# Half of a Strassen-Winograd feed-forward's weight sums moved from GpSimd to accumulating DMAs, half to VectorE

## Chip, core and metric

One core of one Trainium2 chip runs the whole program. The metric is the device time of one execution in microseconds (us), the median of three. TensorE is called PE below, VectorE DVE, ScalarE ACT, GpSimd POOL, and SyncE, which only issues transfers, SP.

## What is computed

The reference is two transformer blocks over x of 512 positions by 1024 features in fp32, with causal recurrences and several kinds of attention. The change touches the feed-forward of the first block, which stands in it twice:

```
def _swiglu(h, w_gate, w_up, w_down):
    g = h @ w_gate
    u = h @ w_up
    return (silu(g) * u) @ w_down        # 1024 -> 2816 -> 1024
x = x + mix                               # recurrent mixer (layer 0), stick-breaking attention (layer 1)
x = x + _swiglu(rmsnorm(x) , ...)
```

## The kernel before

**Layout.** Everything is transposed: features on the 128 partitions, the 512 positions along the free axis. X holds the 1024 features as 8 chunks. A full-precision product is three PE passes over fp32r operands: each operand is split in a high part (ACT copies it to fp32r: Wh, Hh, Fh, Yh) and a low part (DVE subtracts: Wl, Hl, Fl, Yl), and PE adds high by low, low by high and high by high.

**Two output units at a time.** An output unit is 128 features of the gate or of the up projection. A pair h is one gate unit and the up unit of the same features. Instead of 2 by 2 by 2 block products, a pair is computed with seven (Strassen-Winograd): the weights are cut in A11, A12 (gate, two halves of the 1024 inputs) and A21, A22 (up), the activations in B11, B12, B21, B22 (inputs by halves of the positions). Weight operands of the seven products are A11, A12, A22 and four sums: S1 = A21 + A22, S2 = S1 - A11, S3 = A11 - A21, S4 = A12 - S2. T1 to T4 are the matching sums of activations, made once for each norm. One block product is 4 steps of 3 matmuls with 256 columns, so a pair has 84 matmuls. The 44 pairs come in four parts: gu0a (12 pairs), gu0b (10), gu1a (12), gu1b (10). Each is followed by its down projection, down0a and so on. The a parts begin while the output projection of the mixer (rg_out, sb_out) runs out, with the norm; the b parts begin behind a down projection.

**Who does what for pair g+1 while PE multiplies pair g.** SP's `load_pairs` (L393 to L413) loads the gate and the up row, 512 KB each, in raw_w (parity 1 in Wr, parity 0 in scr). POOL's `weight_sums` (L527 to L553) makes S3, S1, S2, S4 in this order, one tensor_tensor of 128x512 each; the first two read both rows, and each waits until its target is free, which DVE's low splits tell it. `sum_hi` (ACT, L1378 to L1386) makes the high part of A (A11 and A12 in one, 128x1024), A22, S1 to S4, and `sum_lo` (DVE, L1997 to L2002) the low part. `split_at` gives the count of splits at which each block is ready. DVE also evacuates the products: four reads of 128x256 (`read` L2086, `rows_right` L2096), a scaling (`rows_left` L2091), act by up (L2102) and the low part of the result (L2106).

**Order on DVE in `iteration(g)`** (L2112 to L2160), which is written out by hand: rows_right(g-2), S4(g-1) low, act_by_up(g-2), S3(g+1) low, Y low (g-2), first read of g, A(g+1) low, third_read(g-1), S1(g) low, rows_left(g-1), A22(g+1) low, second read of g, S2(g+1) low. On PE (`pair`) the order is S3, A12, A11, S1 of the pair before, A22, S2, S4 of the pair before; S2 waits for the first read, S4 for third_read.

**Norm.** In the eight steps m of the mixer's output projection (`out_proj`, ACT L1388, DVE L2037) DVE adds unit m to X, ACT and DVE make the quarters T1 to T4 of chunk m in fp32 and split them (`even_quarters`, `odd_quarters`, `even_lo`, `odd_lo`), ACT squares the chunk, and POOL's `add_square` (L518 to L525) adds the squares up. The inputs' halves are taken as even and odd chunks, so each half is complete only at the end.

Of the kernel before, what the change touches and what calls it, by code (L numbers as in the profile page):

```python
# [16 lines left out]
ACT = mybir.ActivationFunctionType  # L17
ALU = mybir.AluOpType
# [115 lines left out]
OUT_KC = {"rg_out": KD, "sb_out": KD, "even_out": MIXC, "odd_out": MIXC}  # L134
PAIR_OUT = {"gu0a": "rg_out", "gu0b": "down0a", "gu1a": "sb_out", "gu1b": "down1a"}
# [35 lines left out]
def program(nc, a):  # L171
    with ExitStack() as ctx:
# [47 lines left out]
        def part(off, n, w):  # L220
# [38 lines left out]
        raw_w = [(part(7168, KD, P), part(8192, KD, P)),  # L259
                 tuple(Wr[:, q, 0:KD * P].rearrange("p (k c) -> p k c", k=KD) for q in range(2))]  # L260
        raw_rows = raw_w
        raw_w = [[r.rearrange("p (j e) c -> p e j c", e=2) for r in two] for two in raw_w]
        sum3, sum2 = scr[:, 9216:9728], scr[:, 9728:10240]
# [17 lines left out]


# [64 lines left out]
        sum_ok, p2_ok, dc_ok, e_ok = sem("sum_ok"), sem("p2_ok"), sem("dc_ok"), sem("e_ok")  # L347
        dh_ok, rt1_ok = sem("dh_ok"), sem("rt1_ok")
# [6 lines left out]

        def block4(t):
            return t.rearrange("p (j c) -> p j c", j=4)
# [9 lines left out]
        def weight_source(tag, par):  # L367

            if tag == "A":
                return raw_w[par][0]  # L370
            if tag == "A22":
                return raw_w[par][1][:, 1]
            return block4({"S1": sum1[par], "S2": sum2, "S3": sum3, "S4": sum4[par]}[tag])

        def weight_view(w, tag):

            return weights(w, tag).rearrange("p (e j c) -> p e j c", e=2, j=4) if tag == "A" else block4(weights(w, tag))
# [3 lines left out]
        def _(sp):  # L381
# [11 lines left out]
            def load_pairs(name, b, row, pairs):  # L393

                p0, landed = PAIR0[name], 8 * b - SKIP[name]
                rows = a[f"w{KD}"].rearrange("u p (k c) -> u p k c", c=P)

                def load_pair(h, par):
                    for q in range(2):
                        sp.wait_ge(w_in[q], 16 * h + landed)  # L400
                        if h == 0:
                            if name.endswith("a"):
                                sp.wait_ge(x_ok, X0[PAIR_OUT[name]] + 1)
                            else:
                                sp.wait_ge(w_lo, b - 7)
                        elif h == 1:
                            sp.wait_ge(w_lo, b - 1 + q)
                        else:
                            sp.wait_ge(w_lo, b + 2 + q if h == 2 else 6 * h + (b - 12 + 2 * q))
                            sp.wait_ge(sum_ok, 4 * h + (4 * p0 - 4))  # L410
                        sp.dma_start(raw_rows[par][q], rows[2 * h + (row + q)]).then_inc(w_in[q], 16)
                for h in range(pairs):
                    load_pair(h, h % 2)  # L413
# [23 lines left out]
            for name, kc, n in STREAM:  # L437
# [12 lines left out]
                if name in DOWNS:  # L450
                    gu = name.replace("down", "gu")
                    p0, b, pairs = PAIR0[gu], UNIT0[gu], kc
                    sp.wait_ge(w_lo, b + 6 * pairs - 5)
                    sp.wait_ge(sum_ok, 4 * (p0 + pairs))
                    sp.dma_start(Wr[:, 0, 0:kc * P], w[row]).then_inc(w_in[0], 16)
                    sp.wait_ge(w_lo, b + 6 * pairs)
                    sp.dma_start(Wr[:, 1, 0:kc * P], w[row + 1]).then_inc(w_in[1], 16)
                    it0 = 1
                if name in ("rg_out", "sb_out"):
                    load(u0, 0, w[row])  # L460
                    load(u0 + 1, 1, w[row + 1])
                    sp.wait_ge(w_hi, u0 + 1)
                    sp.dma_start(place(Wr, CORNER, KD), w[row + 2].rearrange("p (s c) -> p s c", s=2)).then_inc(w_in[0], 16)
                    load(u0 + 3, 1, w[row + 3])
                    it0 = 2
# [12 lines left out]
        def _(pool):  # L478
# [39 lines left out]
            def add_square(norm, m):  # L518

                pool.wait_ge(sq_ok, SQUARES[norm] + m + 1)  # L520
                if m == 0:
                    pool.tensor_copy(acc[:, :], sq[:, 0, :]).then_inc(acc_ok, 1)
                else:
                    pool.wait_ge(acc_ok, SQUARES[norm] + m)
                    pool.tensor_tensor(acc[:, :], acc[:, :], sq[:, m % 2, :], ALU.add).then_inc(acc_ok, 1)  # L525

            def weight_sums(name, h, par, steps=(0, 1, 2, 3)):  # L527

                b, p0 = UNIT0[name], PAIR0[name]
                gate, up = raw_w[par]  # L530
                lo_at = {"S3": 6 * h + (b - 7), "S1": 6 * h + (b - 5), "S2": 6 * h + (b - 3), "S4": 6 * h + (b - 2)}
                if isinstance(h, int) and h < 2:
                    corner = b - 5 if name.endswith("a") else b - 1 + h
                    lo_at = {"S3": b + 1 if h else b - 7, "S1": corner, "S2": b + 4 if h else b - 7, "S4": b - 7}
                done = 4 * h + 4 * p0
                for step in steps:
                    if step == 0:
                        landed = 16 * h + (8 * b - SKIP[name] + 16)
                        pool.wait_ge(w_in[0], landed)
                        pool.wait_ge(w_in[1], landed)  # L540
                        pool.wait_ge(w_lo, lo_at["S3"])
                        pool.tensor_tensor(block4(sum3), gate[:, 0], up[:, 0], ALU.subtract).then_inc(sum_ok, 1)
                    if step == 1:
                        pool.wait_ge(w_lo, lo_at["S1"])
                        pool.tensor_tensor(block4(sum1[par]), up[:, 0], up[:, 1], ALU.add).then_inc(sum_ok, 1)
                    if step == 2:
                        pool.wait_ge(w_lo, lo_at["S2"])
                        pool.wait_ge(sum_ok, done + 2)
                        pool.tensor_tensor(block4(sum2), block4(sum1[par]), gate[:, 0], ALU.subtract).then_inc(sum_ok, 1)
                    if step == 3:  # L550
                        pool.wait_ge(w_lo, lo_at["S4"])
                        pool.wait_ge(sum_ok, done + 3)
                        pool.tensor_tensor(block4(sum4[par]), gate[:, 1], block4(sum2), ALU.subtract).then_inc(sum_ok, 1)  # L553

            def ffn(layer, norm):
                for part_, chunks in (("a", FFA), ("b", FFB)):
                    name = f"gu{layer}{part_}"
                    if part_ == "a":
                        for m in range(6):
                            add_square(norm, m)  # L560
                        weight_sums(name, 0, 0, (0, 1))
                        add_square(norm, 6)
                        weight_sums(name, 0, 0, (2, 3))
                        add_square(norm, 7)
                    else:
                        weight_sums(name, 0, 0)
                    weight_sums(name, 1, 1)
                    with pool.Fori(1, chunks // 2) as it:
                        for par in range(2):
                            weight_sums(name, 2 * it + par, par)  # L570

            ffn(0, "ffn0")
            ffn(1, "ffn1")

# [767 lines left out]
        def _(act):  # L1342
# [35 lines left out]
            def sum_hi(name, h, tag, par, used):  # L1378

                p0 = PAIR0[name]  # L1380
                if tag in ("A", "A22"):
                    act.wait_ge(w_in[tag == "A22"], 16 * h + (8 * UNIT0[name] - SKIP[name] + 16))
                else:
                    act.wait_ge(sum_ok, 4 * h + (4 * p0 + {"S3": 1, "S1": 2, "S2": 3, "S4": 4}[tag]))
                act.wait_ge(w_used, used)
                act.activation(weight_view(Wh, tag), weight_source(tag, par), ACT.Copy).then_inc(w_hi, 1)  # L1386

            def out_proj(name, norm, pairs_in=None):  # L1388
# [6 lines left out]
                for m in range(KD - 2 if norm == "final2" else KD):  # L1395
# [14 lines left out]
                    if pairs_in:  # L1410
                        j, e = m // 2, m // 2 % 2
                        act.wait_ge(x_ok, x0 + m + 1)
                        if m % 2 == 0:
                            both = tE[e].rearrange("p (a b) -> p a b", b=256)[:, 0:3:2, :]
                            act.activation(both, X[:, m, :].rearrange("p (a b) -> p a b", b=256), ACT.Copy,
                                           scale=v_col(norm, m)).then_inc(xe2_ok, 1)
                            if m == 6:
                                sum_hi(pairs_in, 0, "A", 0, u0 + 7)
                            square(norm, m, X[:, m, :])
# [4 lines left out]
                        else:  # L1424
                            chunk_hi(Hh[:, m, :], X[:, m, :], v_col(norm, m))
                            square(norm, m, X[:, m, :])
# [482 lines left out]
        def _(dve):  # L1909
# [87 lines left out]
            def sum_lo(name, h, tag, par):  # L1997
# [3 lines left out]
                dve.tensor_tensor(weight_view(Wl, tag), weight_source(tag, par), weight_view(Wh, tag).bitcast(F32), ALU.subtract)\  # L2001
                    .then_inc(w_lo, 1)  # L2002

# [853 lines left out]
```

## Time and profile before

| | us |
|---|---|
| median of 3 runs (lowest, highest) | 1937.99 (1937.77, 1940.19) |
| the profiled execution | 1939.89 |
| its span, first to last instruction | 1938.2 |
| PE, DVE, ACT, POOL busy in it | 1877.3, 1377.6, 944.6, 452.3 |
| transfers | 174.02 MB, mean 90 GB/s |

The profiled execution took 1.7 us more than its span and 1.9 more than the median. Durations on DVE overlap a little in the trace: the next instruction's row starts some 0.07 before the end of the one before, so what an instruction costs its engine is read as the distance of two starts.

### The profile page before, as it was taken

What the parts mean: (1) busy time and instruction counts of PE and PEld (TensorE: products, weight loads), DVE (VectorE), ACT (ScalarE), POOL (GpSimd) and SP (SyncE); (2) the same over time, 40 slices, a digit from 0 to 9 for tenths busy, and PEclk for the clock granted to TensorE, in tenths of its full rate; (3) what the DMA queues carried; (4) which work ended last, traced back from release to release, by engine and by line L of the source; (5) the groups of instructions that cost most, each with busy time, mean ns of one, the idle gap of its engine ahead of it and who ended that gap; (6) DMA issues with size and microseconds to landing.
All of it is one profiled execution on the core that took longest, in us unless ns stands there. A gap on an engine that the chain in (4) does not pass through costs nothing.

```text
span 1938.2 us, 30375 instructions
## 1 busy us (share of the span) xinstructions
PE 1877.3 (97%) x10662; PEld 1563.2 (81%) x10662; DVE 1377.6 (71%) x2106; ACT 944.6 (49%) x1573; POOL 452.3 (23%) x426
## 2 busy tenths in 40 slices
PE   9999799999999999979999999999999999999998
PEld 7787689989988777769988998876777887777777
DVE  7687899739965677689964996666667565656553
ACT  6476466415543444546632555345655344444442
POOL 3011555126400000056502530000002045341000
PEclk9999899999999999989999999999999999999999
DMA  7334233233222222223223313211123233232322
GB/s 255 101 96 127 86 98 97 82 114 89 78 96 79 74 61 62 63 87 98 87 98 98 108 57 119 77 55 60 52 86 95 87 89 85 76 87 80 93 82 76
DMA packets 53874, 174.02 MB, mean 90 GB/s; under 512 B 7392, under 2 KB 15712, under 8 KB 53776
## 3 DMA queue, kind: packets, MB, share of 16 engines
q1 hardware_dynamic: 47408, 162.62, 26.8%
q0 software_dynamic: 6368, 10.13, 2.3%
q8 instruction: 57, 0.93, 0.2%
q14 instruction: 41, 0.34, 0.1%
HBM read 168.51 MB, written 4.21 MB: 89 GB/s over the span
## 4 chain that ended last, share of the span: by engine, by line
PE 73%; DVE 11%; issue 4%; ACT 1%; DVEq 0%; ACTq 0%
PE ps L656 15%; PE ps L658 15%; PE ps L657 15%; DVE Wl L2001 4%; PE ps L944 3%; PE tr L910 3%; PE ps L742 3%; PE ps L744 3%; PE ps L743 3%; PE sc L742 2%; PE sc L744 2%; PE sc L743 2%; PE sc L867 2%; DVE Fl L2001 1%; DVE gs L2086 1%
## 5 line engine op out<-in xcount | busy, mean ns | idle before, releaser
L656 PE MATMUL ps<-Hl,Wh 128*128 128x512 f32 x784 | 329.1, 420 | 0.0
L1354 ACT ACTIVATE Wh<-Wr 128x1024 fp32r<-128x1024 f32 (+2 forms) x172 | 195.6, 1139 | 258.7 <-PE ps L658 226.9
L658 PE MATMUL ps<-Hh,Wh 128*128 128x512 f32 x784 | 307.7, 392 | 0.0
L657 PE MATMUL ps<-Hh,Wl 128*128 128x512 f32 x784 | 307.1, 392 | 0.0
L1915 DVE TENSOR_TENSOR Wl<-Wr,Wh 128x1024 fp32r<-128x1024 f32 (+2 forms) x172 | 231.3, 1345 | 102.3 <-ACT Wh L1354 100.8
L656 PE MATMUL ps<-Yl,Wh 128*128 128x512 f32 (+1 forms) x648 | 254.1, 392 | 11.1 <-DVE Wl L1915 7.7
L657 PE MATMUL ps<-Yh,Wl 128*128 128x512 f32 (+1 forms) x648 | 250.8, 387 | 0.0
L658 PE MATMUL ps<-Yh,Wh 128*128 128x512 f32 (+1 forms) x648 | 250.4, 386 | 0.0
L656 PEld LDWEIGHTS ps<-Hl,Wh 128*128 128x128 f32 x784 | 147.8, 188 | 40.3 <-issue 11.1
L742 PE MATMUL ps<-Hl,Wh 128*128 128x256 f32 x528 | 153.8, 291 | 24.9 <-DVE gs L2086 18.8
L2001 DVE TENSOR_TENSOR Wl<-scr,Wh 128x512 fp32r<-128x512 f32 (+1 forms) x132 | 174.5, 1326 | 1.0 <-ACT Wh L1386 1.0
L658 PEld LDWEIGHTS ps<-Hh,Wh 128*128 128x128 f32 x784 | 147.5, 188 | 33.2
L657 PEld LDWEIGHTS ps<-Hh,Wl 128*128 128x128 f32 x784 | 148.1, 189 | 25.8 <-issue 0.5
L656 PEld LDWEIGHTS ps<-Yl,Wh 128*128 128x128 f32 x648 | 122.8, 189 | 38.9 <-issue 9.7
L744 PE MATMUL ps<-Hh,Wh 128*128 128x256 f32 x528 | 150.1, 284 | 0.0
L743 PE MATMUL ps<-Hh,Wl 128*128 128x256 f32 x528 | 150.1, 284 | 0.0
L658 PEld LDWEIGHTS ps<-Yh,Wh 128*128 128x128 f32 x648 | 122.9, 190 | 24.7
L657 PEld LDWEIGHTS ps<-Yh,Wl 128*128 128x128 f32 x648 | 123.0, 190 | 24.0 <-issue 0.7
L1386 ACT ACTIVATE Wh<-scr 128x512 fp32r<-128x512 f32 (+1 forms) x132 | 91.6, 699 | 99.4 <-PE ps L744 72.7
L742 PEld LDWEIGHTS ps<-Hl,Wh 128*128 128x128 f32 x528 | 101.6, 192 | 33.0 <-DVE gs L2086 20.7
L1565 ACT ACTIVATE scr<-tr 128x768 f32<-128x768 f32 (+1 forms) x96 | 72.4, 754 | 74.9 <-PE tr L910 74.2
L2001 DVE TENSOR_TENSOR Wl<-Wr,Wh 128x1024 fp32r<-128x1024 f32 (+1 forms) x88 | 104.6, 1193 | 4.7 <-ACT Wh L1386 4.5
(405 smaller groups left out, 4326.1 us busy)
## 6 DMA issues: line engine op xcount, KB each, us to landing
Wr<-in_w SPq DMA_DIRECT2D x184, 512.0 KB, 3.6
Wr<-in_w SPq DMA_DIRECT2D x32, 768.0 KB, 4.1
scr<-in_w SPq DMA_DIRECT2D x44, 512.0 KB, 3.6
Wr<-in_w SPq DMA_DIRECT2D x16, 640.0 KB, 3.8
scr<-in_rpb POOLq DMA_DIRECT2D x128, 24.0 KB, 2.1
X<-in_x SPq DMA_DIRECT2D x8, 256.0 KB, 4.2
Wr<-in_wri SPq DMA_DIRECT2D x4, 512.0 KB, 3.5
out_t<-X SPq DMA_DIRECT2D x8, 256.0 KB, 2.5
```

The lines of the kernel that those rows point to most:

```text
L656: pe.matmul(bank[:, 0:n], hi, rl[:, k, :], start=(k == 0), stop=False)
L657: pe.matmul(bank[:, 0:n], lo, rh[:, k, :], start=False, stop=False)
L658: return pe.matmul(bank[:, 0:n], hi, rh[:, k, :], start=False, stop=(k == kc - 1))
L742: pe.matmul(out, hi[:, cs], tl, start=(begins and j == 0), stop=False, skip_group_check=True)
L743: pe.matmul(out, lo[:, cs], th, start=False, stop=False, skip_group_check=True)
L744: mm = pe.matmul(out, hi[:, cs], th, start=False, stop=(j == 3), skip_group_check=True)
L910: mm = pe.transpose(tr[:, h, n * P:(n + 1) * P], Pb[:, 2 * (t % 2) + h, n * P:(n + 1) * P], ident[:, :])
L1354: act.activation(place(Wh, slot, kc), place(Wr, slot, kc), ACT.Copy).then_inc(w_hi, 1)
L1386: act.activation(weight_view(Wh, tag), weight_source(tag, par), ACT.Copy).then_inc(w_hi, 1)
L1565: act.activation(PT.rearrange("p h (c q) -> p h c q", c=4)[:, :, cs[0]:cs[0] + n, b * P:(b + 1) * P], tr[:, :, 0:n * P].rearrange("p h (c ...
L1915: dve.tensor_tensor(place(Wl, slot, kc), place(Wr, slot, kc), place(Wh, slot, kc).bitcast(F32), ALU.subtract)\
L2001: dve.tensor_tensor(weight_view(Wl, tag), weight_source(tag, par), weight_view(Wh, tag).bitcast(F32), ALU.subtract)\
```

## The change

S1 and S3 are no longer computed by an engine. SP loads one operand into the place of the sum (sum1 with A21, sum3 with A11), and POOL issues a DMA with `accum_op=ALU.add` that reads the other operand from HBM again and adds it to what lies in SBUF (A22 to sum1, A21 to sum3). [...] S2 and S4 are made by DVE, in `second_sum` and `fourth_sum`. `add_square` of the two feed-forward norms moves from POOL to DVE. The halves of the inputs are now chunks 0 to 3 and 4 to 7, so that a sum is one contiguous half row; the mixer's output units are taken in the order CHUNK so that the pairs of halves still come side by side. sum3 has two buffers instead of one. Of the up row only the right half is loaded plainly. DVE gets two small tensor_scalar instructions for negated gains.

```
+CHUNK = [0, 4, 1, 5, 2, 6, 3, 7]
-        sum3, sum2 = scr[:, 9216:9728], scr[:, 9728:10240]
+        raw_a = [scr[:, 7168:8192], Wr[:, 0, 0:2 * S]]
+        raw_22 = [scr[:, 8192:8704], Wr[:, 1, 0:S]]
+        sum3, sum2 = [scr[:, 8704:9216], scr[:, 9216:9728]], scr[:, 9728:10240]
+        def summed(p0, h, par):
+            return 8 * (h - par) + (8 * p0 + 16)
# SP, load_pairs: for each pair
+                def blocks(h, par):
+                    gate, up = rows[2 * h + row], rows[2 * h + (row + 1)]
...
+                        sp.wait_ge(w_lo, b + lo_at["S3"])          # of pair h - 2
+                    sp.dma_start(sum3[par], gate[:, 0:S]).then_inc(s3_in[par], 16)
...
+                        sp.wait_ge(w_lo, b + lo_at["A"])
+                        sp.wait_ge(sum_ok, 2 * (p0 + h - 1))
+                    sp.wait_ge(w_in[0], 16 * h + landed)
+                    sp.dma_start(raw_a[par], gate).then_inc(w_in[0], 16)
...
+                        sp.wait_ge(w_lo, b + lo_at["A22"])
+                    sp.wait_ge(w_in[1], 16 * h + landed)
+                    sp.dma_start(raw_22[par], up[:, S:2 * S]).then_inc(w_in[1], 16)
+                blocks(0, 0)
                 for h in range(pairs):
...
+                        sp.wait_ge(w_lo, b + split_at(h - 2, pairs)["S1"])
+                    sp.dma_start(sum1[par], rows[2 * h + (row + 1)][:, 0:S]).then_inc(s1_in[par], 16)
+                    if h + 1 < pairs:
+                        blocks(h + 1, 1 - par)
# POOL: the four tensor_tensor of weight_sums go, and
+                def third(h, par):
+                    pool.wait_ge(s3_in[par], summed(p0, h, par))
+                    pool.dma_start(sum3[par], a[f"w{KD}"][2 * h + (row + 1)][:, 0:S], accum_op=ALU.add).then_inc(s3_ok[par], 16)
+                third(0, 0)
+                for h in range(pairs):
+                    par = h % 2
+                    pool.wait_ge(s1_in[par], summed(p0, h, par))
+                    pool.dma_start(sum1[par], a[f"w{KD}"][2 * h + (row + 1)][:, S:2 * S], accum_op=ALU.add).then_inc(s1_ok[par], 16)
+                    if h + 1 < pairs:
+                        third(h + 1, 1 - par)
# DVE
+            def second_sum(name, h, par):
...
+                dve.wait_ge(s1_ok[par], summed(p0, h, par))
...
+                dve.tensor_tensor(sum2, sum1[par], raw_a[par][:, 0:S], ALU.add).then_inc(sum_ok, 1)
+            def fourth_sum(name, h, par):
+                dve.wait_ge(sum_ok, 2 * h + (2 * PAIR0[name] + 1))
+                dve.tensor_tensor(sum4[par], sum2, raw_a[par][:, S:2 * S], ALU.add).then_inc(sum_ok, 1)
@@ iteration
                     if more:
+                        second_sum(name, g + 1, 1 - par)
                         sum_lo(name, g + 1, "A", 1 - par)
...
                     if more:
+                        fourth_sum(name, g + 1, 1 - par)
                         sum_lo(name, g + 1, "S2", 1 - par)
@@ odd_quarters: one scalar_tensor_tensor of 512 columns becomes two of 256
@@ out_proj
+                    if pairs_in and nrm:
+                        add_square(nrm, m)
```

## Rows read from the trace of the kernel before

**Rows 1.** The page, its head and busy times.

```profile
span 1938.2 us, 30375 instructions
PE 1877.3 (97%) x10662; PEld 1563.2 (81%) x10662; DVE 1377.6 (71%) x2106; ACT 944.6 (49%) x1573; POOL 452.3 (23%) x426
```

**Rows 2.** Busy time by window: begin, length, engines, granted PEclk, DMA share, GB/s.

```profile
222.00:260.00 38.00, 29.95 (x202) 27.85 (x201) 32.36 (x35) 19.89 (x32) 24.76 (x16) 0.91 0.27 83
...
236.00:353.00 117.00, 109.34 (x855) 105.28 (x856) 114.56 (x136) 70.92 (x112) 63.93 (x42) 0.99 0.27 81
```

**Rows 3.** Timeline of PE's weight loads, one pair: start, us, what, [idle before].

```profile
330.42 0.19 PEld L743 LDWEIGHTS ps<-Eh,Wl 128*128 128x128 f32 x1
330.54 0.19 PEld L744 LDWEIGHTS ps<-Eh,Wh 128*128 128x128 f32 x1
...
331.46 0.19 PEld L742 LDWEIGHTS ps<-Hl,Wh 128*128 128x128 f32 x1 [0.74 <-DVE gs L2086]
...
342.52 0.19 PEld L742 LDWEIGHTS ps<-Hl,Wh 128*128 128x128 f32 x1 [0.73 <-DVE gs L2086]
```

**Rows 4.** Timeline of DVE in the same pair, and after POOL's last sum.

```profile
326.47 1.78 DVE L2001 TENSOR_TENSOR Fl<-scr,Fh 128x512 fp32r<-128x512 f32 x1
...
329.11 1.97 DVE L2001 TENSOR_TENSOR Wl<-Wr,Wh 128x1024 fp32r<-128x1024 f32 x1
...
331.34 0.67 DVE L2001 TENSOR_TENSOR Wl<-Wr,Wh 128x512 fp32r<-128x512 f32 x1
...
332.27 1.78 DVE L2001 TENSOR_TENSOR Wl<-Wr,Wh 128x512 fp32r<-128x512 f32 x1
...
350.29 0.68 DVE L2106 TENSOR_TENSOR Yl<-ht,Yh 128x512 fp32r<-128x512 f32 x1
350.89 0.41 DVE L2086 TENSOR_TENSOR sq<-ps,rstd 128x256 f32<-128x256 f32 x1
351.23 1.21 DVE L2001 TENSOR_TENSOR Wl<-Wr,Wh 128x1024 fp32r<-128x1024 f32 x1
352.36 0.41 DVE L2086 TENSOR_TENSOR gs<-ps,acc 128x256 f32<-128x256 f32 x1
```

**Rows 5.** Timeline of POOL, one sum of the same pair.

```profile
332.09 1.41 POOL L545 TENSOR_TENSOR Wr<-scr 128x512 f32<-128x512 f32 x1 [2.09 <-DVE Wl L2001]
```

**Rows 6.** Timeline of PE's weight loads at the start of gu0a.

```profile
226.65 0.28 PEld L742 LDWEIGHTS ps<-Hl,Wh 128*128 128x128 f32 x1 [3.43 <-issue]
...
234.12 0.19 PEld L742 LDWEIGHTS sc<-El,Fh 128*128 128x128 f32 x1 [1.53 <-DVE El L2035]
...
241.54 0.19 PEld L742 LDWEIGHTS sc<-El,Fh 128*128 128x128 f32 x1 [1.03 <-DVE Fl L2001]
...
247.95 0.19 PEld L742 LDWEIGHTS ps<-Hl,Wh 128*128 128x128 f32 x1 [1.58 <-DVE Wl L2001]
```

**Rows 7.** DMA issues: queue, count, KB each, median us from issue to landing.

```profile
scr<-in_w SPq DMA_DIRECT2D x44, 512.0 KB, 3.6
...
out_t<-X SPq DMA_DIRECT2D x8, 256.0 KB, 2.5
scr<-d_rel POOLq DMA_DIRECT2D x8, 192.0 KB, 3.6
...
scr<-d_memk POOLq DMA_DIRECT2D x2, 512.0 KB, 5.2
...
scr<-in_rope POOLq DMA_DIRECT2D x1, 512.0 KB, 4.3
```

**Rows 8.** Timelines of POOL and DVE in the neighbourhood attention's first bias loads.

```profile
1489.88 8.42 POOL L611 DMA_DIRECT2D scr<-in_rpb  x16 [81.37 <-PE sc L915]
```

**Rows 9.** Timeline of DVE in the same stretch.

```profile
1492.64 0.68 DVE L2291 TENSOR_TENSOR Yl<-acc,Yh 128x512 fp32r<-128x512 f32 x1
...
1494.35 1.76 DVE L1915 TENSOR_TENSOR Wl<-Wr,Wh 128x1536 fp32r<-128x1536 f32 x1 [1.02 <-ACT Wh L1354]
```

**Rows 10.** Timeline of SP's queue in the pair of rows 3.

```profile
331.14 3.30 SPq L411 DMA_DIRECT2D Wr<-in_w  x2
```

More of the change, by code:

```diff
@@ L280, in program @@
         ps += [ctx.enter_context(nc.psum_tensor(f"ps{i}", [P, S], F32)) for i in range(6, 8)]
+        first_row, _rows = {}, {}
+        for _name, _k, _n in STREAM:
+            first_row[_name] = _rows.get(_k, 0)
+            _rows[_k] = first_row[_name] + _n
         def place(w, slot, kc):
@@ L367, in weight_source @@
         def weight_source(tag, par):
[L369 to L377, printed above, removed]
+            return {"A": raw_a[par], "A22": raw_22[par], "S1": sum1[par], "S2": sum2, "S3": sum3[par], "S4": sum4[par]}[tag]
+        def summed(p0, h, par):
+            return 8 * (h - par) + (8 * p0 + 16)
         @block.sync
@@ L393, in load_pairs @@
             def load_pairs(name, b, row, pairs):
[L395 to L411, printed above, removed]
@@ L460, in _ @@
                     load(u0, 0, w[row])
-                    load(u0 + 1, 1, w[row + 1])
+                    load(u0 + 1, 1, w[row + CHUNK[1]])
                     sp.wait_ge(w_hi, u0 + 1)
-                    sp.dma_start(place(Wr, CORNER, KD), w[row + 2].rearrange("p (s c) -> p s c", s=2)).then_inc(w_in[0], 16)
-                    load(u0 + 3, 1, w[row + 3])
-                    it0 = 2
+                    sp.dma_start(place(Wr, CORNER, KD), w[row + CHUNK[2]].rearrange("p (s c) -> p s c", s=2)).then_inc(w_in[0], 16)
+                    for m in range(3, KD):
+                        load(u0 + m, m % 2, w[row + CHUNK[m]])
+                    continue
                 with sp.Fori(it0, n // 2) as it:
@@ L516, in _ @@
             store_mem_v(1)
[L518 to L570, printed above, removed]
@@ L572, in _, with weight_sums @@
-            ffn(0, "ffn0")
-            ffn(1, "ffn1")
+            def weight_sums(name):
+                p0, row, pairs = PAIR0[name], first_row[name], FFA if name.endswith("a") else FFB
+                def third(h, par):
[3 more added lines that the diff above has]
+                for h in range(pairs):
+                    par = h % 2
+                    pool.wait_ge(s1_in[par], summed(p0, h, par))
+                    pool.dma_start(sum1[par], a[f"w{KD}"][2 * h + (row + 1)][:, S:2 * S], accum_op=ALU.add).then_inc(s1_ok[par], 16)
+                    if h + 1 < pairs:
+                        third(h + 1, 1 - par)
@@ L575, in _ @@
+            for name in ("gu0a", "gu0b", "gu1a", "gu1b"):
+                weight_sums(name)
             pool.wait_ge(w_used, UNIT0["down1b"])
@@ L2000, in sum_lo @@
                 dve.wait_ge(w_hi, b + split_at(h, pairs)[tag])
-                dve.tensor_tensor(weight_view(Wl, tag), weight_source(tag, par), weight_view(Wh, tag).bitcast(F32), ALU.subtract)\
+                dve.tensor_tensor(weights(Wl, tag), weight_source(tag, par), weights(Wh, tag).bitcast(F32), ALU.subtract)\
                     .then_inc(w_lo, 1)
+            def second_sum(name, h, par):
+                p0 = PAIR0[name]
+                if not (isinstance(h, int) and h == 0):
+                    prior = h - 1 if not isinstance(h, int) or h > 1 else 0
+                    dve.wait_ge(w_lo, UNIT0[name] + split_at(prior, 99)["S2"])
+                    dve.wait_ge(sum_ok, 2 * h + 2 * p0)
+                dve.wait_ge(s1_ok[par], summed(p0, h, par))
+                dve.wait_ge(w_in[0], 16 * h + (8 * UNIT0[name] - SKIP[name] + 16))
+                dve.tensor_tensor(sum2, sum1[par], raw_a[par][:, 0:S], ALU.add).then_inc(sum_ok, 1)
+            def fourth_sum(name, h, par):
+                dve.wait_ge(sum_ok, 2 * h + (2 * PAIR0[name] + 1))
+                dve.tensor_tensor(sum4[par], sum2, raw_a[par][:, S:2 * S], ALU.add).then_inc(sum_ok, 1)
             def even_quarters(nrm, m):
@@ L2055, in out_proj @@
                         bank = m if name in ("rg_out", "sb_out") and m < 4 else b0 + m % 2
-                        dve.tensor_tensor(X[:, m, :], X[:, m, :], ps[bank][:, :], ALU.add).then_inc(x_ok, 1)
+                        c = CHUNK[m] if name in ("rg_out", "sb_out") else m
+                        dve.tensor_tensor(X[:, c, :], X[:, c, :], ps[bank][:, :], ALU.add).then_inc(x_ok, 1)
                     if name in ("rg_out", "sb_out") and m == 0:
@@ L2063, in out_proj @@
                     if pairs_in and m == 6:
+                        second_sum(pairs_in, 0, 0)
                         if not nrm:
@@ L2460, in _ @@
             rg_lo(RB - 1)
+            for norm, home in MINUS.items():
+                dve.tensor_scalar(vec[:, VEC[home]:VEC[home] + KD], vec[:, VEC[norm]:VEC[norm] + KD], -1.0, None, ALU.mult)\
+                    .then_inc(neg_ok, 1)
             out_proj("rg_out", "ffn0", "gu0a")
```

70 lines of the change are left out of this document (46 added, 24 removed).

## The prediction

> **What bounds the kernel now.** The page comes first: PE is busy for 97% of the span, so little is to be had from anything else [rows 1]. But the change touches one stage only, so I read that stage by windows: over the pairs of gu0a DVE is busy for 114.56 of 117 us, PE for 109.34, POOL for 63.93 [rows 2]. There DVE, not PE, is full. The timeline of PE's weight loads says what that costs. Loads follow each other every 0.12 us (330.42 to 330.54), so the 84 matmuls of a pair need 10.08; yet the same product begins at 331.46 and at 342.52, 11.06 apart [rows 3]. The missing 0.98 is PE waiting for a read by DVE before S4 (0.92 between two loads), and a shorter wait before S2. I count 28 of the 44 pairs with this wait: 8 in each a part, 6 in each b part.
>
> Why is DVE full? Its timeline shows a low split of 128x512 at 0.67 (S1, 331.34) and the next, same shape, at 1.78 (A22, 332.27) [rows 4]. In between POOL's sum begins at 332.09 [rows 5]. Each of POOL's four sums in a pair holds one DVE instruction up. Behind POOL's last sum the same list runs free, and distances of starts there give net prices [rows 4]: 0.60 for 512 columns (350.29 to 350.89), 0.34 for 256 (to 351.23), 1.13 for 1024 (to 352.36). A pair has seven, five and one of these: 7 x 0.60 + 5 x 0.34 + 1.13 = 7.03. The other 4.03 of 11.06 are POOL's.
>
> **The change, part by part.**
>
> *POOL's sums go, two come to DVE.* 7.03 + 2 x 0.60 = 8.23 us of DVE in a pair, under PE's 10.08. I laid DVE's list against PE's: the first read can be done 2.3 us before S2 needs it, third_read, now with second_sum and A low ahead of it, 1.6 before S4. So both waits go: 28 x 0.98 = **-27**.
>
> *The fronts of gu0a and gu1a.* PE waits 3.43 for the first half of the inputs, 1.53 for the second, 1.03 for S3 of pair 1 and 1.58 for the second read [rows 6]. All stand behind DVE work that POOL holds up, about 1.1 each time; I replay the list with free prices and the new instructions. X's chunk 6 is then added 2.5 us sooner and the first wait goes; of the 1.53 some 0.7 go, the third goes, of the fourth 1.4; and 2.1 of small waits in the next two pairs: 3.4 + 0.7 + 1.1 + 1.4 + 2.1 = 8.7, twice: **-18**. The granted clock is 0.91 over 222 to 260 [rows 2], with two stretches of half speed that begin behind these waits; without them some 3 come back: **-3**. Last pairs of the parts and starts of the b parts have waits for DVE of 0.3 to 0.6: **-2**.
>
> *add_square on DVE.* 16 at 0.60, in steps where POOL's adds cost DVE 1.1 each: nothing net, inside the -18. If that cover is gone they cost up to 10.
>
> *Signs, CHUNK, contiguous halves, the split scalar_tensor_tensor (+0.1 x 8), two negations:* same operations on other addresses; nothing, covered by DVE's slack of 1.9 in a pair, at most 2 without it.
>
> *SP and POOL queues.* SP issues five loads in a pair for two, at about 0.33 each; its queue starts 0.06 behind its release (A low ends 331.08, SP 331.14 [rows 4, 10]) and otherwise idles. Transfers grow from 1.0 to 1.75 MB in a pair; the DMA share of 0.27 [rows 2] becomes about 0.5. Issuing from POOL does not hold DVE: beside POOL's issues from 1489.88 to 1498.30 [rows 8] a 512 instruction takes 0.68 and a 1536 one 1.76 [rows 9].
>
> *The new chain.* This is the uncertain term. sum1 of pair g+2 may be loaded only when S1 low of g is done; the load lands, POOL issues the accumulating DMA, it lands, second_sum, A low and third_read of the next iteration follow, then S1 low of g+1, which releases the next load. So the chain has one period to run in:
> c = L1 + L2 + hand-offs 0.3 + DVE 2.8 (0.66 + 1.13 + 0.34 + 0.68).
> L1, a load of 256 KB by SP: 2.5 (a store of that size) to 3.6 (512 KB) [rows 7]; I take 2.7, near the row of its size, plus a little for sum3's load right behind. L2, 256 KB through POOL with an addition, is in no row. From below: 192 KB plain takes 3.6 with others ahead, and a first one some 0.4 less, so 3.2. From above: 512 KB plain in company, 5.2 [rows 7], and a row that nothing excludes could be longer, 6. I take 4.3, the 512 KB plain row, as the addition moves two operands. That gives c = 10.1. The gate and up loads for the pair after, 768 KB, are issued about 2.3 after sum1's and run against the accumulation: +0.2. **c = 10.3**, against 10.08. 36 pairs follow the chain: 36 x 0.22 = **+8**. At each part's start it begins late: by the replay of gu0b's start S1 low of pair 0 ends 5.5 before the moment at which second_sum of pair 2 would have to begin for PE's S4 not to wait, so S4 waits L1 + L2 + 0.3 - 5.5 = 1.8, four times: **+7**.
>
> On that price the Trainium skill speaks against the change: "Collectives: The Full Stack" (The bandwidth ceiling: the fold count and why AG ≠ RS ≠ AR) has an adding DMA read two sources through one ring, so that it moves at half the rate of a copy. No row here shows an addition; by that rule L2 is that of a 512 KB copy, the 4.3 taken above.
>
> **Sum.** -27 - 18 - 3 - 2 + 8 + 7 = -35 on the profiled execution's 1939.9: 1905. The median of the runs lies 1.9 lower, so **1903**. The formula for other prices: -50 + 4 (L1 + L2 - 5.2) + 36 max(0, c - 10.08). It is back at zero at c of 11.15, L1 + L2 of 8.0.
>
> **Rivals.**
> *A, slower: the sum1 chain becomes the bound.* Place: second_sum waits for s1_ok, and everything behind it on DVE, third_read above all, for which PE waits. Price: 40 us for each us of c. It decides from c = 11.15 up. With L1 = 3.6 and L2 = 5.2, both rows, c = 11.9 and -50 + 14 + 65 = +29: 1967. With 3.0 and 5.5 c is 11.6: +18, 1956. For it: every row of L2 is a guess by size, three DMAs compete. Against: between the bursts the engines stand idle. Chance 0.22.
> *B, the chain has room.* L2 = 3.2 to 3.6: c = 9.2 to 9.6, no stall in the loop, starts cost 2 to 4: -47, 1891. For it: the row of 192 KB. Chance 0.25. The skill's "DMA: Bandwidth & Descriptors" (Anatomy of one DMA — SWDGE (gpsimd) path) would put this DMA at 2.0 + bytes/436e3, an estimate of 2.6, and so speaks for B; the rows for 192 KB are a us longer, so it gets no more.
> *C, POOL's hold on DVE stays in another form* (descriptor writing, DMA writes into buffers being read), or add_square and the new order undo the fronts: about what it was, 1930 to 1942. Against: rows 8 and 9. Chance 0.06.
> *The forecast,* c within about 0.6 above PE's 10.08: 1893 to 1923. Chance 0.47.
>
> **Numbers.** Faster by over 0.2% (about 4 us, what a measurement of this kernel can tell): forecast, B and half of C, less a margin: 0.74. Slower by over 0.2%: A, 0.22. Within: 0.04. The range takes in B's 1890, the forecast, and of A all but its end: 1887 to 1960.
>
> **What would show it.** Right: no POOL tensor_tensor between 190 and 1165; all 512-column low splits at 0.67 to 0.69; DVE busy about 8.2 in a pair; pairs 10.1 to 10.4 apart; the load that waited 3.43 waits under 1. The accumulating DMA lands 4.3 behind its issue. If c is over: DVE idles ahead of second_sum, released by a DMA, and PE's S4 waits for third_read as before, with a period equal to c. I am wrong if pairs stand over 11 apart, if low splits still take 1.78, or if the accumulating DMA lands after more than 5.3.

## The result, and the profile after

The kernel after the change takes 1965.58 us in the median of four runs (1964.4 to 1969.48), the kernel before beside it 1937.88 (1937.24 to 1940.19). The ratio is 1.0144, 95% interval 1.0127 to 1.0162: slower by 27.7 us, where I had forecast 35 us faster. It is rival A that came true, with its place and almost its price. The profiled execution is the one of 1964.4 us, with a span of 1962.7, 24.5 more than the span before.

The page after, its head, busy times and the rows of the DMA issues (count, KB each, median us to landing), to be held against [rows 1, 7]:

```profile
span 1962.7 us, 30196 instructions
PE 1875.2 (96%) x10662; PEld 1567.3 (80%) x10662; DVE 1279.7 (65%) x2220; ACT 951.7 (48%) x1573; POOL 233.6 (12%) x322
...
Wr<-in_w SPq DMA_DIRECT2D x66, 256.0 KB, 3.0
...
scr<-in_w POOLq DMA_DIRECT2D x44, 256.0 KB, 6.5
Wr<-in_w POOLq DMA_DIRECT2D x44, 256.0 KB, 5.7
```

DVE is busy for 98 us less and POOL for 219 less, as the change intends, and the time is longer all the same. The last two rows are S3's and S1's accumulations; I had taken 4.3 for the latter.

The same two windows of busy time by engine as [rows 2] (begin and length, then PE, PEld, DVE, ACT, POOL, granted PEclk, DMA share, GB/s):

```profile
222.00:260.00 38.00, 29.48 (x211) 27.95 (x209) 25.87 (x47) 19.02 (x30) 5.26 (x6) 0.91 0.56 133
236.00:353.00 117.00, 100.42 (x801) 98.60 (x800) 81.43 (x144) 71.08 (x108) 16.82 (x19) 0.97 0.61 146
```

Over the pairs of gu0a DVE fell from 114.56 to 81.43 us, so it is no longer full. PE fell too, from 109.34 to 100.42: both wait for something that is on no compute engine. The waits over 230 to 560 us name it (us in total, times, longest):

```profile
DVE scr L2001 <- DMA Wr<-in_w: 47.6, 17, 5.6
...
PE ps L728 <- DVE gs L2096: 29.7, 16, 6.0
```

L2001 is second_sum. L2096 is the helper of the first three reads; the one that PE waits for writes gs right behind A low, and is the third read. PE waits for it as in [rows 3], but it now waits, through A low, for second_sum, and that for S1's accumulation. One turn of the loop stands in the timelines of SP, POOL and DVE (start, us, what, [idle before]):

```profile
309.66 0.33 SPq L434 DMA_DIRECT2D Wr<-in_w  x1
...
322.01 0.33 SPq L434 DMA_DIRECT2D Wr<-in_w  x1
...
333.78 0.33 SPq L434 DMA_DIRECT2D Wr<-in_w  x1
```

```profile
312.90 0.87 POOL L554 DMA_DIRECT2D Wr<-in_w  x1 [9.77 <-DMA Wr<-in_w]
313.52 1.16 POOL L548 DMA_DIRECT2D scr<-in_w  x1
```

```profile
319.22 0.69 DVE L2001 TENSOR_TENSOR scr<-Wr,scr 128x512 f32<-128x512 f32 x1 [3.21 <-DMA Wr<-in_w]
319.83 1.22 DVE L1989 TENSOR_TENSOR Wl<-scr,Wh 128x1024 fp32r<-128x1024 f32 x1
320.96 0.42 DVE L2096 TENSOR_TENSOR gs<-ps,rstd 128x256 f32<-128x256 f32 x1
321.30 0.68 DVE L1989 TENSOR_TENSOR Wl<-Wr,Wh 128x512 fp32r<-128x512 f32 x1
```

SP loads sum1 at 309.66, POOL issues the addition at 312.90 (3.2 later), second_sum begins at 319.22 (6.3 later), A low, the third read and S1 low follow without a gap, and at 322.01 SP's next load starts. The turns are 12.35 and 11.77 us long. Every step of the chain that the prediction wrote down is there, in its order; its length is another. Two of the three signs that the prediction named against itself are there (turns over 11 apart, a landing after more than 5.3); the third, low splits at 1.78, is not.

At the start of gu0a the weight loads show the chain's late beginning, ahead of S4 of pair 0 (249.57). That is not the place of the last wait in [rows 6]: the 1.58 stood ahead of S1 of pair 0, where the kernel after waits 0.46 (239.06). At S4 of pair 0 the kernel before waited 0.73:

```profile
253.41 0.19 PEld L742 LDWEIGHTS ps<-Hl,Wh 128*128 128x128 f32 x1 [0.73 <-DVE Wl L2001]
```

The kernel after:

```profile
227.95 0.19 PEld L728 LDWEIGHTS sc<-El,Fh 128*128 128x128 f32 x1 [0.80 <-DVE El L2041]
...
249.57 0.29 PEld L728 LDWEIGHTS ps<-Hl,Wh 128*128 128x128 f32 x1 [6.14 <-DVE Wl L1989]
249.74 0.34 PEld L729 LDWEIGHTS ps<-Hh,Wl 128*128 128x128 f32 x1
249.96 0.33 PEld L730 LDWEIGHTS ps<-Hh,Wh 128*128 128x128 f32 x1
```

Behind this wait the clock granted to PE is 0.50, the lower of its two levels (1.2 and 2.4 GHz); the window, columns as above:

```profile
250.00:254.00 4.00, 4.00 (x20) 4.00 (x20) 3.64 (x8) 1.44 (x2) 0.82 (x2) 0.50 0.65 154
```

**Where the time went.** The fourth read of a pair by DVE (sq<-ps,rt, L2096 before, L2106 after, L2109 in the experiment e1_s1_on_dve) marks each pair's progress. The first and the last of a part, with stretches worked out from them, in us:

| stretch of layer 0 | before | after | e1_s1_on_dve |
|---|---|---|---|
| first read of gu0a at | 257.55 | 252.65 | 247.50 |
| first to last (12th) read of gu0a | 114.14 | 121.08 | 108.03 |
| last of gu0a to first of gu0b | 82.24 | 85.45 | 81.04 |
| first to last (10th) read of gu0b | 92.06 | 98.95 | 86.69 |

So the change gives 4.9 us in the front, loses 6.9 in gu0a, 3.2 ahead of gu0b and 6.9 in it: 12.1 lost in layer 0, and read the same way 11.7 in layer 1, 24 of the 24.5 between the two spans. The column on the right is the same kernel without the loop; there each of the four stretches is shorter than before.

### The profile page after: what moved, and what is told of

The parts are those of the page before. It is cut to its first block and busy times, and to the rows that moved or that the text cites. A ratio compares the mean times of both kernels' runs of the same rounds, so it can differ in the third digit from the quotient of the medians.

```text
span 1962.7 us, 30196 instructions
## 1 busy us (share of the span) xinstructions
PE 1875.2 (96%) x10662; PEld 1567.3 (80%) x10662; DVE 1279.7 (65%) x2220; ACT 951.7 (48%) x1573; POOL 233.6 (12%) x322
## 5 line engine op out<-in xcount | busy, mean ns | idle before, releaser
L642 PE MATMUL ps<-Yl,Wh 128*128 128x512 f32 (+1 forms) x648 | 253.9, 392 | 11.4 <-DVE Wl L1903 8.2
L644 PEld LDWEIGHTS ps<-Hh,Wh 128*128 128x128 f32 x784 | 147.1, 188 | 32.9
L643 PEld LDWEIGHTS ps<-Hh,Wl 128*128 128x128 f32 x784 | 147.8, 188 | 25.7 <-issue 0.5
L729 PEld LDWEIGHTS ps<-Hh,Wl 128*128 128x128 f32 x528 | 103.7, 196 | 0.3
L730 PEld LDWEIGHTS ps<-Hh,Wh 128*128 128x128 f32 x528 | 103.8, 197 | 0.0
```

The source lines that it names most:

```text
L642: pe.matmul(bank[:, 0:n], hi, rl[:, k, :], start=(k == 0), stop=False)
L643: pe.matmul(bank[:, 0:n], lo, rh[:, k, :], start=False, stop=False)
L644: return pe.matmul(bank[:, 0:n], hi, rh[:, k, :], start=False, stop=(k == kc - 1))
L729: pe.matmul(out, lo[:, cs], th, start=False, stop=False, skip_group_check=True)
L730: mm = pe.matmul(out, hi[:, cs], th, start=False, stop=(j == 3), skip_group_check=True)
```

## The experiments

My theory after the result: S1's accumulation takes longer than I gave it, and only because one period must hold the whole loop does this cost time. Rivals: the accumulations slow down something else (SP's loads, DVE), S3's accumulation is the culprit, or the two additions on DVE are dearer than 0.6.

**e1_s1_on_dve** takes S1's addition away from the DMA and gives it to DVE; the summand is loaded anyway, for A22. S3 stays with the DMA.

```
-  pool.wait_ge(s1_in[par], ...)
-  pool.dma_start(sum1[par], ... [:, S:2 * S], accum_op=ALU.add).then_inc(s1_ok[par], 16)
   (second_sum)
-  dve.wait_ge(s1_ok[par], summed(p0, h, par))
+  dve.wait_ge(s1_in[par], summed(p0, h, par))
+  dve.wait_ge(w_in[1], ...)
+  dve.tensor_tensor(sum1[par], sum1[par], raw_22[par], ALU.add).then_inc(s1_ok[0], 1)
+  dve.wait_ge(s1_ok[0], h + (p0 + 1))
```

> S1 is added by VectorE (one more tensor_tensor of 128x512 in a pair, in front of second_sum) instead of by an accumulating DMA; S3 is still accumulated by DMA. Theory, the sum1 chain is the bound of the changed kernel: its leg through GpSimd (5.7 us) goes, the chain falls to about 3.0 + 0.2 + 3.4 = 6.6 us, VectorE has 8.8 us of work in a pair, and pairs stand at TensorE's 10.1 us: 1892 us, 1886 to 1902. Rival, the added transfers or the denser VectorE list slow the pairs in general: pairs stay above 10.8 us, 1925 us or more.

Measured: 1896.06 us (1895.08 to 1896.34) against 1938.65, ratio 0.9778 (0.9762 to 0.9794). One of the two accumulations, taken away, turns 28 us of loss into 43 of gain, although DVE has one more addition in each pair. The third rival, dear additions, is answered by the kernel after itself: second_sum begins at 319.22 and the next instruction at 319.83, 0.61 later, and no low split of 512 columns there takes over 0.69. The windows:

```profile
222.00:260.00 38.00, 34.53 (x272) 32.76 (x271) 33.91 (x61) 23.09 (x38) 3.46 (x4) 1.00 0.51 134
236.00:353.00 117.00, 115.09 (x939) 113.69 (x940) 101.28 (x179) 78.64 (x121) 7.83 (x9) 1.00 0.51 138
```

PE is busy for 115.09 of 117 us. The DMA share is 0.51, for 0.61 after, and S3's accumulation still takes 4.8 us here (7.8 at most). ScalarE waits for it twice, 2.6 us in all, and nothing else does.

**e2_late_second** keeps all the work and both accumulations. It moves second_sum of the next pair from ahead of A low to just ahead of fourth_sum, behind S1 low of this pair.

```
                     if more:
-                        second_sum(name, g + 1, 1 - par)
                         sum_lo(name, g + 1, "A", 1 - par)
 ...
                     if more:
+                        second_sum(name, g + 1, 1 - par)
                         fourth_sum(name, g + 1, 1 - par)
```

> One line moved: second_sum comes right in front of fourth_sum instead of in front of A's low split; all four DMAs are as in the changed kernel. Theory, it is the closed loop and not the length of the DMA that costs: S1's low split no longer stands behind second_sum, the sum has some 12 us from the release of its load where 9.2 are needed, and pairs stand at 10.1 us although the accumulating DMA still lands about 6 us behind its issue: 1892 us, 1887 to 1905. Rival, the accumulating DMAs are late wherever their result is asked for: a wait of 1.5 us or more stays in each pair, 1950 us or more.

Measured: 1900.05 us (1898.23 to 1901.1), ratio 0.9798 (0.9782 to 0.9814). The row of the accumulating DMA:

```profile
  DVE scr L2001: 4.1, 5
...
DMA to landing us min/median/max: 3.9/6.1/7.9
```

S1's accumulation is slower than in the kernel after (6.1 for 5.7), and the kernel 66 us faster. DVE waited for it 5 times, 4.1 us in all; in the kernel after that was 35 times and 93.4 us. One turn in gu0b, from the timelines of SP, POOL and DVE:

```profile
456.48 0.33 SPq L434 DMA_DIRECT2D Wr<-in_w  x1
...
459.70 0.88 POOL L554 DMA_DIRECT2D Wr<-in_w  x1 [7.15 <-DMA Wr<-in_w]
...
467.89 0.68 DVE L2001 TENSOR_TENSOR scr<-Wr 128x512 f32<-128x512 f32 x1
```

From the load to its second_sum there are 11.4 us, and the two DMAs with their hand-offs need some 9.4 of them (3.2 and 6.1); in the kernel after second_sum began 9.56 behind the load, the moment the data was there. And the release of the next load (S1 low) no longer stands behind second_sum in its iteration, so the loop closes over two periods and not over one. This separates the theory from every rival by which the accumulations cost time by being there.

**e3_plain_copy, e5_small_loads, e12_plain_small** ask why it is 5.7. The first drops the additions: both DMAs copy the up block over the gate block's part. The second leaves the additions and takes away the company.

```
 (e3)   pool.dma_start(sum1[par], ...[:, S:2 * S])          # no accum_op, the same for sum3
 (e5) + few = 16 if h > 1 else 2 * S                        # 16 of 1024 columns
        sp.dma_start(raw_a[par][:, 0:few], gate[:, 0:few])
      + few = 16 if h > 1 else S                            # 16 of 512 columns
        sp.dma_start(raw_22[par][:, 0:few], up[:, S:S + few])
```

> The accumulating DMAs of GpSimd become plain copies of the same size at the same places, so S1 and S3 are no longer sums (the output is another one). Theory A, the addition is what makes them long: they land 4.3 us or less behind their issue instead of 5.7 and 6.5, pairs stand at 10.3 us, about 1905 us. Theory B, the company is what makes them long (five loads and two of these in each pair): they land 5.0 us or more behind the issue, 1940 us or more.

> Left out: from the third pair of a part on, the gate block (512 KB) and the right half of the up block (256 KB) are loaded only in their first 16 columns, so the weights of those pairs are partly old ones and the outputs other ones; every wait, sum and DMA instruction stays. Theory: S1's accumulation takes 5.7 us and not the 4.5 of the quiet stretch because it shares the sixteen DMA engines with the 768 KB of loads of the same pair. Then it falls to 4.5 to 4.9 here, sum1's first load to 2.4, the loop from load to load by about 1.0 us in 36 pairs and the start of the parts by 1 each: 1925 to 1935 us. Rival 1, the length is the accumulation's own: 5.5 to 5.8 still, and 1960 to 1967 us. Rival 2, the matmuls wait for something else than sum1's loop: the accumulation is shorter and the time within 5 us of 1965.

> e3_plain_copy and e5_small_loads in one: the two sums by DMA are plain copies of the up block over the gate block's part (the additions are left out), and the loads of the gate block and of the up block's right half bring only 16 columns from the third pair on; outputs other ones. With the kernel after (5.7 us with addition and company), e3_plain_copy (4.7 without the addition) and e5_small_loads (4.2 without the company) it is the fourth corner. If the two prices add up: 5.7 - 1.0 - 1.5 = 3.2 us, sum1's loop below 10.3, and 1893 to 1903 us. If one hides in the other (both are the same wait for a DMA engine): 4.0 to 4.3 us and 1905 to 1915.

Measured, one execution each (the four executions of the kernel after lie within 5.1 us): 1935.75, 1914.43 and 1900.45 us. The accumulating (or copying) DMA of S1 in each, from issue to landing, e3, e5 and e12 in this order:

```profile
  DVE scr L2001: 58.1, 33
...
DMA to landing us min/median/max: 2.8/4.7/5.5
```

```profile
  DVE scr L2003: 39.6, 30
...
DMA to landing us min/median/max: 3.9/4.2/4.8
```

```profile
  DVE scr L2003: 10.0, 6
...
DMA to landing us min/median/max: 2.8/3.0/5.0
```

| S1's DMA, median us (time of the kernel) | loads of 768 KB beside it | loads cut to 16 columns |
|---|---|---|
| with the addition | 5.7 (1965.6) | 4.2 (1914.4) |
| plain copy | 4.7 (1935.8) | 3.0 (1900.5) |

The addition costs 1.0 to 1.2 us and the company 1.5 to 1.7, and the two prices add up. That is the whole distance from 3.0 to 5.7. So e3 lands between its two theories (4.3 or less, 5.0 or more); e5 frees more than I expected (4.5 to 4.9 us, and 1925 to 1935 for the kernel); e12 comes as the sum of the two prices had it.

What the company does stands in the DMA views of the kernel after, packets, MB and share of the sixteen engines by queue; q1 is SP's, q0 POOL's. First the 2.1 us from the issue at 312.90, then 315.00 to 318.60:

```profile
q1 hardware_dynamic: 171, 0.55, 82.5%
q0 software_dynamic: 1, 0.00, 0.7%
...
q0 software_dynamic: 247, 0.46, 80.8%
q1 hardware_dynamic: 108, 0.20, 19.1%
```

For the first 2.1 us the engines work on SP's loads. In the median of 40 pairs POOL's queue moves its first packet 2.1 us behind the issue in the kernel after and 1.6 in e5, 2.2 in e3 and 1.2 in e12: 0.5 to 1.0 of the company's price is this later start, and the rest falls behind it.

The times follow the latency while the loop binds: 51 us for 1.5 us from after to e5, 30 for 1.0 from after to e3, or 30 to 34 for each us, where I had put 40 (36 pairs and four starts); L1, the load ahead of it, is 2.9 to 3.0 in all three. Shorter than 4.0 us it pays less, since with L1 of 3.0 and 3.1 for the rest the loop is then shorter than PE's 10.08: from e5 to e12, 1.2 us bring only 14.

**e4_s3_left_out** leaves out S3's accumulation (S3 is then the gate block's part alone), to see whether it delays S1's.

```
-  third(0, 0)
-  if h + 1 < pairs: third(h + 1, 1 - par)
-  act.wait_ge((s1_ok if tag == "S1" else s3_ok)[par], ...)
+  act.wait_ge((s1_ok if tag == "S1" else s3_in)[par], ...)
```

> The accumulation of S3 is left out (S3 is the loaded A11 alone, so the output is another one); S1's stays. Theory B, company: with 256 KB less read and no second GpSimd DMA behind it, S1's lands about 0.8 to 1.0 us sooner than 5.7, the period falls by as much, 36 x 0.9 = 32 us less: about 1933 us. Theory A, the addition itself: S1's stays at 5.5 us or more, 1955 us or more.

Measured: 1955.57 us, one execution, S1's accumulation at 5.6 in the median, and DVE waiting for it 37 times, 86.4 us. The second accumulation, issued 0.6 us behind the first, costs it 0.1 us and the kernel 10. It is not the culprit: S1's is still at 5.6, as the theory of the addition had asked (5.5 or more), though by e3 and e5 the addition is less than half of the distance from 3.0. By the fourth reads, of the 8.8 us between the two spans 3.3 lie ahead of the first read of gu0a and 1.3 ahead of that of gu1a, 1.6 between the parts and 2.4 within them. Why there was not followed.

**e6_pool_reads and e7_pool_writes** test the other half of the prediction, that POOL's additions held DVE in the kernel before. Both start from e1_s1_on_dve and give POOL idle work in 28 of the 44 pairs, an addition of spare tiles twice in the one, a fill with zeros twice in the other.

```
+  if 2 <= h < pairs - 2:
+      for _ in range(2):
+          pool.tensor_tensor(spare, other, other, ALU.add)     # e6
+          pool.memset(spare, 0.0)                               # e7
```

> Added to e1_s1_on_dve: in 28 of the 44 pairs GpSimd adds a spare 512-column tile twice into another, as it did four times a pair in the kernel before; nobody waits for the result. Theory (GpSimd's hold on VectorE is what bound the kernel before): a VectorE split of 512 columns beside it takes 1.7 to 1.8 us, not 0.68, VectorE's work of a pair rises from about 8.5 by 2.2 to about 10.7, and these pairs take 0.4 to 1.0 us more: 1907 to 1925 us. Rival, the hold costs nothing where VectorE has slack: splits lengthen and the time stays at 1894 to 1899. Rival 2, there is no hold by an addition of whole rows: splits stay 0.68.

> As e6_pool_reads, but GpSimd fills the spare tile with zeros twice a pair instead of adding: it writes as much and reads nothing. Theory: the hold belongs to GpSimd's reading (what held VectorE in the kernel before were additions), so splits stay at 0.68 us and the time at 1894 to 1899. Rival, any work of GpSimd on the memory holds VectorE: splits of up to 1.7 us and 1905 to 1925.

Measured: 1939.57 and 1897.95 us, one execution each. Two additions that nobody waits for undo the gain: 43.5 us in 28 pairs, 1.55 in each, well over the 0.4 to 1.0 that I expected. Nor does S3's DMA, which stands behind them in POOL's queue, explain it: between 255 and 335 us DVE waits for no DMA, and ScalarE for 1.0 us as in e1. The timelines of POOL and of DVE in e6, then of both in e7:

```profile
285.73 2.82 POOL L548 TENSOR_TENSOR scr<-scr 128x512 f32<-128x512 f32 x2
```

```profile
285.50 2.15 DVE L2003 TENSOR_TENSOR Fl<-scr,Fh 128x512 fp32r<-128x512 f32 x1
287.57 1.52 DVE L2133 TENSOR_TENSOR Yl<-ht,Yh 128x512 f32 x1
```

```profile
290.33 1.46 POOL L548 MEMSET scr<- 128x512 f32 x2
```

```profile
290.61 0.69 DVE L2129 TENSOR_TENSOR ht<-sq,gs 128x512 f32<-128x512 f32 x1 [1.41 <-ACT sq L1465]
291.21 0.69 DVE L2003 TENSOR_TENSOR Fl<-scr,Fh 128x512 fp32r<-128x512 f32 x1
```

Two additions of 1.4 us each hold two DVE instructions by 1.5 and 0.8 us. The fills leave the same split at 0.69. They take 0.73 each for 1.4, but in the whole of e7 no low split of 512 columns in the four parts takes over 0.69. So the hold comes with POOL's reading and not with its writing. The Trainium skill, "SBUF — State Buffer" (SBUF: two separate sides), says this of the two engines' shared ports: an instruction of VectorE with two inputs in the memory is shut out only by one of GpSimd that reads it. Both runs agree.

**e8_best, e11_late_unrolled, e10_squares_on_pool** look for the best version and for the term that I had set to nothing. e8 is e1 with both sums one step later and ScalarE's loop over pairs written out; e11 is e2 with the same loop written out; e10 is e8 with add_square of the two fronts back on POOL.

```
 (e8, e11, ACT)
-  with act.Fori(1, pairs // 2 - 1) as it:
-      for par in range(2): iteration(2 * it + par, par)
+  for g in range(2, pairs - 2): iteration(g, g % 2)
 (e8, DVE: second_sum(name, g + 1, 1 - par) moves from ahead of A low to ahead of A22 low)
 (e10)
+  pool.wait_ge(sq_ok, ...); pool.tensor_tensor(acc, acc, sq[:, m % 2], ALU.add)   # 16 steps, a copy first in each front
+  dve.wait_ge(acc_ok, SQUARES[norm] + KD)                                         # once a front
```

> e1_s1_on_dve with two more edits: the first and second sums of the next pair move behind the left rows (one read and one split later), and ScalarE's loop over pairs is written out, so that no table load stands at its head. Theory: in e1_s1_on_dve the pairs are 10.32 us apart, as every second one loses 0.45 us for VectorE that stands behind the two table loads of 1.28 us at the head of ScalarE's loop; without them the pairs come to 10.1 apart, 36 times 0.2: 1887 to 1892 us. Rival, the 0.45 is VectorE's own load of work and not ScalarE's: 1894 to 1899, or more where S1 comes too late now.

> e2_late_second (S1 still added by DMA, VectorE's second sum moved back to stand before the fourth) with ScalarE's loop over pairs written out, so that no two table loads stand at the head of each second pair. Theory: in e2_late_second the reads are 9.3 and 11.45 us apart in turn, 10.36 on the mean, and the long one is the one with the table loads; without them 10.1 on the mean, 8 pairs by 0.26 in the parts with a loop: 1892 to 1896 us, level with e8_best (1894). Rival, the long pair belongs to S1's DMA (even buffers later than odd): 1898 to 1901, unchanged.

> e8_best with the sums of squares of the two norms ahead of the parts a back on GpSimd, as in the kernel before (16 additions of 512 columns, and a wait of VectorE for the last). My prediction costed this move at nothing net: VectorE is rid of 8 times 0.68 us a part and is held 8 times by 0.6 to 1.1. By that 1892 to 1897 us, no difference from e8_best's 1894. Rival 1, the holds are worth more where the front's chain runs through VectorE (two splits of e6_pool_reads took 1.47 and 0.83 more): the two fronts 2 to 5 us longer each, 1898 to 1904. Rival 2, VectorE's own additions were the dearer: 1886 to 1891.

Measured: e8 1894.17 us (1893.45 to 1894.37), ratio 0.9768 (0.9752 to 0.9785); e11 1893.77 (1892.26 to 1895.13), ratio 0.9768 (0.9751 to 0.9784); e10 1895.69 (1893.91 to 1896.51), ratio 0.9777 (0.976 to 0.9793).

For e8 I had expected 1887 to 1892, a gain of some 7 us on e1; it is 2, and the two intervals overlap. The two table loads in e1, and the wait that I blamed on them:

```profile
265.71 1.28 ACT L1374 ACT_TABLE_LOAD   x1
...
267.66 1.28 ACT L1452 ACT_TABLE_LOAD   x1
```

```profile
275.33 0.19 PEld L726 LDWEIGHTS ps<-Hl,Wh 128*128 128x128 f32 x1 [0.45 <-DVE gs L2099]
```

The wait is there only three times in gu0a (275.33, 295.96, 316.60) and never in gu0b, where ScalarE makes no table load between 440 and 525 us and the first six distances of e1's reads are already 10.06 to 10.12. I had multiplied it over 36 pairs. In e8 these waits are gone, but ahead of S1 of gu0a's pair 0 it waits 1.60 us (240.48), where e1 has 0.74 and 1.10 (236.27 and 244.62) at two other places of the start.

In e11 the same edit took 6 us off e2, as expected, and S1's accumulation in it takes 6.6 us in the median, 0.9 more than in the kernel after, in a kernel 72 us faster:

```profile
  DVE scr L2000: 4.1, 4
...
DMA to landing us min/median/max: 3.9/6.6/7.3
```

e10 shows no difference from e8 by its interval: add_square is worth nothing net, as the prediction had it. The best versions, e8 and e11, cannot be told apart; both beat the kernel before by 2.3%, and the kernel after by about 71 us.

## Why the prediction was wrong

**The step that failed** is the size of L2. The prediction says "I take 4.3, the 512 KB plain row, as the addition moves two operands", and adds 0.2 for the 768 KB of loads that run against it. Measured: 5.7. The addition by itself was priced about rightly: without company it takes 4.2 (e5), near my 4.3. The company, which I gave 0.2, costs 1.5. With L1 at 3.0 (2.9 for sum1's loads alone; I took 2.7) and the rest of the chain at 3.1 as put, c is 3.0 + 5.7 + 3.1 = 11.8 for my 10.3; the reads of the kernel after stand 11.68 apart in gu0a and 11.86 in gu0b (nine and seven pairs). Against e1, the same kernel without the loop, the stretches from first to last read of the four parts are 49 us longer in the kernel after, and the stretches ahead of the parts 18. So my +8 for the loop was 49, some 1.4 for each of 36 pairs and not 0.22, and my +7 for the starts was 18. My mistake was to take the nearest row by size from stretches where the DMA engines had little to do, while I had worked out myself that the change doubles their share in this stretch, from 0.27 to about 0.5 (0.61 after).

- *POOL's sums go, -27:* right. All low splits of 512 columns in the kernel after take 0.68 to 0.69, as the prediction asked, and e6 brings the hold back. Freed of the loop alone (e1), the stretch from first to last read shrinks by 6.1 us in gu0a and 5.4 in gu0b (the table above), 23 in both layers; in e8, with ScalarE's loop written out too, it is 28 in both.
- *Fronts, -18:* right. e1 reaches its first read 10.05 us sooner than before, and the way from gu0b's last read to gu1a's first is 8.9 shorter; with the clock's -3 I had 21 for both. The kernel after keeps 4.9 of it and gives the rest back at the start of the part.
- *Clock, -3:* right where the waits went: the granted clock in 222 to 260 is 1.00 in e1. In the kernel after it is 0.91 as before, since another wait took their place. It falls to 0.50 at each of the four starts, within this wait or right behind it, and at none of them in e1. No run parts its price from that of the wait.
- *add_square, nothing net:* right (e10).
- *Start of the parts, +7 (1.8 each):* too small. PE waits 6.14 us ahead of S4 of pair 0 in gu0a, 4.04 in gu0b, and 6.15 and 4.16 in layer 1 (timeline of PE's weight loads). By my formula, L1 + L2 + 0.3 - 5.5 with 3.0 and 5.7, it would be 3.5, so L2 is only a part of the miss; the rest stays open.
- *Signs, CHUNK, the split scalar_tensor_tensor, SP's and POOL's queues:* nothing seen; e1 contains them all but S1's DMA, and e2 all. (With ALU.add the kernel after forms S3 = A11 + A21, S2 = S1 + A11 and S4 = A12 + S2, and the up product comes out negated.) SP issues four loads in a pair, not five: L434, L412, L419 and L425 in its timeline.
- *The formula:* with the measured L1 and L2 it gives -50 + 14 + 62 = +26 for the kernel after; measured +27.7. (Its zero at L1 + L2 of 8.0 and rival A leave out the 0.2 that the prediction had added to c for the company; it is left out here too, since the 5.7 holds the company.) But for the free loop it gives -48 (e12, L1 2.7, L2 3.0) where -39 was measured, and -14 for e3 (L1 3.0) where it was -3. So the -50 was some 9 to 11 too good for these two (e8 and e11 reach -44 and -46), and the good fit of the kernel after is partly luck: a too good start and a price for each us of c that is too high cancel.

Rival A at 1967, worked out with L1 = 3.6 and L2 = 5.2, is what happened; the one was too long and the other too short, and their sum of 8.8 for the measured 8.7 is luck. Its chance, 0.22, was too low for a term whose rows ranged from 3.6 to 5.2, in a sum that changes sign at L1 + L2 of 8.0: my values of 2.7 and 4.3 left 1.0 us to it. The Trainium skill's "DMA: Bandwidth & Descriptors" (Anatomy of one DMA — SWDGE (gpsimd) path) put the plain transfer at an estimated 2.6. e12's 3.0, with S3's copy alone beside it, is not far from it. The Trainium skill's "Collectives: The Full Stack" (The bandwidth ceiling: the fold count and why AG ≠ RS ≠ AR) has a reduce step of a ring, which reads two sources, move at half the rate of a copy; 4.2 for 3.0 without SP's large loads goes the same way, and no run here shows the rate by itself.

Open: how the rest of the company's price arises once the first packet has moved, why the starts cost more than the formula has, and what S3's accumulation costs elsewhere (10 us in e4).

## What to carry to other kernels

Before a step goes to another engine or to a DMA, write down the loop that it closes: which wait releases it, what waits for it, and how many periods lie between. Here the same accumulating DMA cost 66 us or nothing, by whether its consumer stood ahead of the instruction that releases the next load. Price a DMA in the company that the change itself brings, not by a row from a quiet stretch. And an engine that is full may be held by another one's reads: two spare additions on GpSimd in 28 pairs cost the 43 us that e1 had gained.

## What the runs showed that I had not expected

- GpSimd is busy longer with issuing an accumulating DMA: 0.87 us for the first of a pair and 1.12 in the median for the one right behind it, for 0.54 with a plain copy of the same size (e3).
- Addition and company add up: 3.0, 4.2, 4.7 and 5.7 us for the four cases of 256 KB.
- GpSimd's additions of 1.4 us hold a DVE split of 0.68 up to 2.15 us; its fills do not hold it.
- After PE's wait of 6.14 us at gu0a's start the weight loads follow each other at 0.17 to 0.22 us for 0.12 [rows 3], with a granted clock of 0.50. That is PE at 1.2 instead of 2.4 GHz. In e1 the wait at that place is 1.10, and the clock is granted in full.
